# A transformer layer with split-precision weights: low parts in pieces, regrouped products, a third pair of split buffers and two moved buffers

## The reference

```
x = layer_norm(x, ...)                                   # "0"
h = x @ w_in + b_in                                      # iq, cbik, qa, kv, qb
out_a = swa_sink_attention(...); out_b = dsa_attention(...)   # top-k selection of keys
x = layer_norm(ALPHA * x + concat(out_a, out_b) @ w_o + b_o)  # "1"
x = layer_norm(ALPHA * x + memory_cross_attention(x, mem, ...))   # "2"
x = layer_norm(ALPHA * x + square(relu(x @ w_up + b_up)) @ w_down + b_down)   # "f"
u = rms_norm(x); x = x + ssd_mixer(u, ...)               # "r0"; 8 groups, 4 chunks each
u = rms_norm(x); x = x + mla_mixer(u, ...)               # "r1"; 16 heads, 8 pairs
return rms_norm(x)                                       # "r2"
```

## Time and profile before

| | |
|---|---|
| median of 3 runs | 1924.07 us (1923.3 to 1924.84) |
| the profiled execution | 1922.4 us, of which span 1920.6 us |
| mean granted PE clock | 0.959 of full speed |
| PE busy | 1763.4 us, 92% |
| PEld (weight loads, beside PE) | 1404.0 us, 73% |
| DVE, ACT, POOL busy | 950.1, 782.3, 621.2 us |
| chain that ended last | PE 72%, DVE 14%, ACT 8%, POOL 2%, issue 2% |

### The profile page before, as it was taken

The page is one execution under the profiler, slowest core; times in us unless marked ns, Lnnn a source line. Parts: engine busy times, 40 slices in busy tenths (PEclk is TensorE's granted clock), DMA queues, the critical chain, the costliest instruction groups (busy, mean ns, idle before and its releaser), DMA issues.

```text
span 1920.6 us, 22716 instructions
## 1 busy us (share of the span) xinstructions
PE 1763.4 (92%) x8994; PEld 1404.0 (73%) x8994; DVE 950.1 (49%) x1871; ACT 782.3 (41%) x1329; POOL 621.2 (32%) x223
## 2 busy tenths in 40 slices
PE   7895789889989999998888999999999999999998
PEld 6674465677778888887766777777778777777776
DVE  5157878353563221214655556345654354545455
ACT  5452343253264232322434444434444544443533
POOL 2323134212114434343124344434441313232320
PEclk9897789989989999999888999999999999999999
DMA  7222010112113222221121111121111212111111
GB/s 279 84 81 88 23 45 23 44 45 84 48 45 110 98 100 88 99 98 55 45 88 66 44 66 66 66 88 61 50 68 66 79 55 70 56 68 67 68 45 44
DMA packets 27408, 137.50 MB, mean 72 GB/s; under 512 B 2815, under 2 KB 9215, under 8 KB 13480
## 3 DMA queue, kind: packets, MB, share of 16 engines
q1 hardware_dynamic: 26248, 135.02, 19.9%
q10 hardware_dynamic: 1056, 1.05, 0.2%
HBM read 133.93 MB, written 2.12 MB: 71 GB/s over the span
## 4 chain that ended last, share of the span: by engine, by line
PE 72%; DVE 14%; ACT 8%; issue 2%; POOL 2%; DMA 1%; SPq 0%; DVEq 0%; ACTq 0%; POOLq 0%
PE ps L1184 70%; ACT whi L1588 2%; PE ps L1188 2%; POOL wlo L2531 1%; DVE STT L2439 1%; DVE XL L2021 1%; DVE SCB L2251 1%; DVE mx L2024 1%; DVE R L2021 1%; DVE m L2249 1%; ACT LG L1589 1%; ACT tmp L1588 1%; DVE tmp L2191 1%; ACT ESG L1588 1%; POOL tmp L2550 1%
## 5 line engine op out<-in xcount | busy, mean ns | idle before, releaser
L2531 POOL TENSOR_TENSOR wlo<-raw,whi 128x2048 fp32r<-128x2048 f32 (+3 forms) x123 | 527.4, 4288 | 1070.0 <-ACT whi L1588 1070.0
L1184 PE MATMUL ps<-XH,whi 128*128 128x512 f32 (+1 forms) x1144 | 446.1, 390 | 9.9 <-DVE XL L2021 4.5
L1184 PE MATMUL ps<-XH,wlo 128*128 128x512 f32 (+1 forms) x1144 | 425.6, 372 | 0.0
L1184 PE MATMUL ps<-XL,whi 128*128 128x512 f32 (+1 forms) x1144 | 425.3, 372 | 0.0
L1588 ACT ACTIVATE whi<-raw 128x2048 fp32r<-128x2048 f32 (+3 forms) x129 | 230.6, 1788 | 165.8 <-PE ps L1184 163.3
L1184 PEld LDWEIGHTS ps<-XH,whi 128*128 128x128 f32 x1144 | 221.2, 193 | 59.8 <-issue 16.5
L1184 PEld LDWEIGHTS ps<-XH,wlo 128*128 128x128 f32 x1144 | 220.8, 193 | 37.2
L1184 PEld LDWEIGHTS ps<-XL,whi 128*128 128x128 f32 x1144 | 221.4, 194 | 36.2 <-issue 2.2
L2121 DVE TENSOR_TENSOR R<-ps,R 128x512 f32<-128x512 f32 (+1 forms) x164 | 94.1, 574 | 288.2 <-PE ps L1184 287.4
L1184 PE MATMUL ps<-BH,whi 128*128 128x512 f32 (+1 forms) x608 | 227.8, 375 | 4.7 <-DVE BL L2461 2.0
L1184 PE MATMUL ps<-BH,wlo 128*128 128x512 f32 (+1 forms) x608 | 217.9, 358 | 0.0
(11 more groups left out here) (296 smaller groups left out, 2848.9 us busy)
## 6 DMA issues: line engine op xcount, KB each, us to landing
raw<-wall SPq DMA_DIRECT2D x108, 1024.0 KB, 4.6
raw<-wall SPq DMA_DIRECT2D x9, 512.0 KB, 3.3
raw<-wall SPq DMA_DIRECT2D x8, 576.0 KB, 3.4
raw<-wall SPq DMA_DIRECT2D x4, 768.0 KB, 4.0
R<-xT SPq DMA_DIRECT2D x1, 2048.0 KB, 13.2
BFL<-scr SPq DMA_DIRECT2D x16, 128.0 KB, 3.4
outT<-R SPq DMA_DIRECT2D x16, 128.0 KB, 1.9
MEM<-memT SPq DMA_DIRECT2D x2, 512.0 KB, 4.3
```

What stands on the lines that cost most here:

```text
L1184: return nc.tensor.matmul(o_, l, r_, start=start, stop=stop, skip_group_check=True)
L2531: tt(wlo[u % NSPL][:, 0:n], raw[u % NRAW][:, 0:n], f32(whi[u % NSPL][:, 0:n]), ALU.subtract).then_inc(S("g_lo"), 1)
```

## The change

Five edits.

1. `NSPL` goes from 2 to 3: a third pair `whi`/`wlo`. Since `split_first` runs over `NSPL` units, it now splits units 0, 1 and 2, all on DVE, and each later `split` is that of unit u + 2 at the place where it was that of u + 1.
2. The subtraction that makes `wlo` is done in pieces of 512 columns (384 where the unit is no multiple of 512), each with its own signal: four instructions for a unit of 2048 columns, on POOL and on DVE.
3. `pj` waits for `whi` alone at first, and for the piece of `wlo` that it needs ahead of each product that reads it. `right` waits for the high or the low part of the input, whichever the product reads.
4. The products of a part are regrouped. In mode "all": high by high for all k's, then high weights by low input for all k's, then low weights for all k's. In the other modes the low weights come ahead of the low input.
5. Addresses. `kv_at` is rounded up to 0 modulo 128, so that the buffers at its start (`KM`, `B2H`, `B2L`, `QCH`, `QCL` among them) begin at 0 modulo 128. `BTK0` and `IDR` move into the space of `RW`, and `st`, `m8` and `mx` into that of `KT`, to make room.

```
-NRAW, NSPL = 3, 2
+NRAW, NSPL = 3, 3
...
-        kv_at = top[0]
+        kv_at = top[0] = (top[0] + 127) // 128 * 128
...
+        def piece(u):
+            return 384 if units[u][1] % 512 else 512
+        def pieces(u):
+            return units[u][1] // piece(u)
...
-            "split": lambda u: ({"a_hi": 1, low[u]: 1}, []),
+            "split": lambda u: ({"a_hi": 1, low[u]: pieces(u)}, []),
...
-            def right(u, k, j):
+            def right(u, k, j, lo):
...
-                        e.wait_ge(*x_low(ep, jj, k))
-                    return XH[:, k, :], XL[:, k, :]
+                        e.wait_ge(*(x_low(ep, jj, k) if lo else on("a_xh", "nm", ep, jj, k // 3, i=k % 3 + 1)))
+                    return (XL if lo else XH)[:, k, :]
...
-                e.wait_ge(*on(low[u], "split", u))
                 h, l = weights(u, K)
                 c = slice(128 * m, 128 * m + 128)
-                for k in range(4 * part, min(4 * part + 4, K) if K == 8 else K):
-                    xh, xl = right(u, k, j)
-                    if key != "wk":
-                        xh, xl = xh[:, span(j)], xl[:, span(j)]
-                    t = three(o_, h[:, k, c], l[:, k, c], xh, xl, k == 0, k == K - 1)
+                ks = range(4 * part, min(4 * part + 4, K)) if K == 8 else range(K)
+                width = units[u][1] // K
+                def product(w, lo, k):
+                    x = right(u, k, j, lo)
+                    return mm(o_, w[:, k, c], x if key == "wk" else x[:, span(j)], k == 0 and w is h and not lo,
+                              k == K - 1 and (w is l if weights_last else bool(lo)))
+                def low_weights(k):
+                    e.wait_ge(*on(low[u], "split", u, i=((k + 1) * width - 1) // piece(u) + 1))
+                    return product(l, 0, k)
+                weights_last = mode == "all"
+                e.wait_ge(*on("a_hi", "split", u))
+                for k in ks:
+                    product(h, 0, k)
+                for last in range(2):
+                    for k in ks:
+                        t = low_weights(k) if weights_last == last else product(h, 1, k)
...
-                n = units[u][1]
+                n = piece(u)
                 e.wait_ge(*on("a_hi", "split", u))
-                tt(wlo[u % NSPL][:, 0:n], raw[u % NRAW][:, 0:n], f32(whi[u % NSPL][:, 0:n]), ALU.subtract).then_inc(S("g_lo"), 1)
+                for i in range(pieces(u)):
+                    c = slice(n * i, n * i + n)
+                    tt(wlo[u % NSPL][:, c], raw[u % NRAW][:, c], f32(whi[u % NSPL][:, c]), ALU.subtract).then_inc(S("g_lo"), 1)
```

More of the change, by code:

```diff
@@ L284, in program @@
         C = sb("C", [128, NCOL])
+        rw_at = top[0]
         RW = sb("RW", [128, NROW])
@@ L319, in program @@
         IW = sb("IW", [128, 4, 8])
-        st = sb("st", [128, 64])
-        m8 = sb("m8", [128, 8])
-        mxs = [sb(f"mx{i}", [128, 16]) for i in range(3)]
+        st = sb("st", [128, 64], at=kt_at + 2048)
+        m8 = sb("m8", [128, 8], at=kt_at + 2304)
+        mxs = [sb(f"mx{i}", [128, 16], at=kt_at + 2336 + 64 * i) for i in range(3)]
         QLS = [sb("QL0", [128, 4, 128]), sb("QL1", [128, 4, 128], at=b_at + 28672)]
@@ L364, in program @@
         XDE = [sb(f"XDE{i}", [128, 256]) for i in range(2)]
-        BTK = [sb(f"BTK{i}", [128, 128]) for i in range(2)]
+        BTK = [sb("BTK0", [128, 128], at=rw_at + 128), sb("BTK1", [128, 128])]
         CBM = [sb(f"CBM{i}", [128, 128]) for i in range(2)]
-        IDR = sb("IDR", [32, 32], F32R)
+        IDR = sb("IDR", [32, 32], F32R, at=rw_at)
         ACH = sb("ACH", [32, T], F32R, at=stat_at)
@@ L2043, in split @@
                     return
-                n = units[u][1]
+                n = piece(u)
                 e.wait_ge(*on("a_hi", "split", u))
-                tt(wlo[u % NSPL][:, 0:n], raw[u % NRAW][:, 0:n], f32(whi[u % NSPL][:, 0:n]), ALU.subtract).then_inc(S("d_lo"), 1)
+                for i in range(pieces(u)):
+                    c = slice(n * i, n * i + n)
+                    tt(wlo[u % NSPL][:, c], raw[u % NRAW][:, c], f32(whi[u % NSPL][:, c]), ALU.subtract).then_inc(S("d_lo"), 1)
             def xsum(k):
```

33 lines of the change are left out of this document (16 added, 17 removed).

## The result

The changed kernel takes 1893.86 us (median of 4 runs, 1893.39 to 1896.34) against 1924.45 for the kernel before on the same chip: ratio 0.9844, 95% interval 0.9827 to 0.9861. It is faster, by 30.6 us. The prediction said 1908 with a range of 1895 to 1920: the direction was right, the gain was about twice the forecast, and the median is 1.1 us outside the range. The profiled execution has a span of 1892.4 us, 28.2 less than before; the sum in the prediction had it 15.0 less. So 13 us are to be explained.

A forecast was written before the change was run, and what follows sets the result against it. PE, busy 92% of the span, was taken as the bound. Span 1920.6 - 21.2 - 5.5 + 11.7 + 2.0 + 1.0 - 3.0 = 1905.6 us, as median 1909.1, with unpriced small locks 1908; range 1895 to 1920.

The forecast's parts named there:

- Scan: DVE's decay product waits for one POOL piece, not a whole split; PE's waits and half clock shrink: -21.2 us.
- the alternation: In the scan's first group DVE and POOL take turns, one instruction each, whatever its length; basis of the 21.2 us.
- POOL keeps the port: Rival: in the scan, a waiting DVE instruction isn't let in between POOL's pieces; 1932 us, chance 0.09.
- given back: Rival: the chain through ACT behind the gated output paces the scan, half of 21.2 us lost; 1919 us, chance 0.12.
- Start: Third unit's split delays DVE's sums over x: PE's mean 9.7 us later, 2.0 us from half clock; +11.7 us.
- Regrouped products: On PE, as many products and weight loads, spacing 0.227 us whichever operand comes next, more waits: cost 0.
- Addresses: Products of 512 columns with moving operands now at 0 modulo 128 run 6.7 ns faster: -3 us, bounds -4 and 0.
- Norms: Four norms: each piece delays one DVE product, gain from waiting for `XH` alone is lost at the sums: +2.0 us.
- The clock: PE's half-clock work behind idle times: 6.8 us come back in the scan, 2.0 us are lost in the start.
- Attention: Less lock on DVE and a later POOL are of one size: +1 us, between -4 and +4.
- Third pair: PE's 4 waits for POOL's `wlo` go, all counted: -5.5 us, bounds 0 and 5.5.
- the start is not late: Rival: PE has other work ahead of the mean, or POOL's pieces miss the sums; 1896 us, chance 0.15.

The follow-up runs named there:

- e2: The changed kernel with each low part made in one instruction per unit again on both engines, all else kept: 1929.51 us, ratio to before 1.0022.
- e5: The kernel before with low parts in pieces of 512 (384) columns alone, PE still waiting for the last piece: 1905.35 us, ratio 0.9894.
- e7: The changed kernel with the third unit's split moved behind the sums over x, and pieces of 1024 columns (or half a unit): 1893.17 us.
- e4: The changed kernel with the three products of one k together again, waits for pieces of the low weights kept: 1900.13 us, ratio 0.9863.
- e9: The changed kernel with the third split behind the sums over x, and POOL's split held until DVE's last sum in three norms: 1873.74 us, ratio 0.9741.
- e10: The kernel before with the new product order alone: whole splits, two pairs, old addresses (some small buffers at new places): 1922.55 us, ratio 0.9984.
- e6: The changed kernel with kv_at left where it falls, at 64 modulo 128, nothing else changed: 1897.89 us.
- e3: The changed kernel with two pairs of split buffers instead of three, the third unit's split back on POOL: 1887.54 us, ratio 0.9794.

## Why the prediction was right in kind and wrong in size

**Scan: right.** -21.2 forecast, -21.7 measured; the alternation read from rows 4 decides. e2 and e5 show that the pieces alone bring it, e7 that it follows the size of a piece. "POOL keeps the port" and "given back" are refuted.

**Start: right** in mechanism and time of each step; 2.2 us too much. PE's product over the sums came 8.8 us late and not 9.7, and behind it 0.7 us more were lost and not 2.0: PE waited 5.5 us for the sums and not 12, having worked meanwhile, in part at half clock (0.83 on the mean over the first 36 us). **Regrouped products: right**, the spacing is unchanged. **Addresses: right in sum.** The 1.9 us between 564 and 886 agree with 288 products of 512 columns by 6.7 ns.

**Norms: the step that failed.** The lock of DVE behind POOL's split was priced as a gain in the scan alone. The prediction said: "By turns each of the four pieces delays one, so the queue's end is not earlier but later by POOL's added 0.5 us. What PE gains by waiting for `XH` alone it loses at the wait for the sums. Four such norms: +2.0." For norms 1 and 2 that is so (+0.05 for norm 1; e4, e9), though PE's wait for the sums of norm 1 is 3.87 us and not over 4, behind 3.0 us of waits for `XH`. I read norm 1 and carried it to all four, and between 886 and 937 that put +0.5 where, apart from the wait for `wlo`, the kernel gained 3.7. In norm f the chain is another one: DVE makes a tile of `R`, ACT squares it into `tmp`, PE adds it up, tile by tile, and there the kernel before had one more site of the kind that I counted only in the scan. Timeline of the kernel before at 909:

```profile
909.20 4.79 POOL L2531 TENSOR_TENSOR wlo<-raw,whi 128x2048 fp32r<-128x2048 f32 x1 [20.10 <-ACT whi L1588]
909.66 4.47 DVE L2017 TENSOR_SCALAR R<-R,C 128x256 f32<-128x256 f32 x1
914.69 2.08 PE L1184 MATMUL ps<-tmp,on1k 128*128 128x256 f32 x4 [4.08 <-ACT tmp L1588]
```

A DVE instruction that takes 0.35 us elsewhere took 4.47, and PE stood still for 4.08. The view of waits names ACT's `tmp` for it, so it hid in a group that I had not opened; only the name `STT` had led me to POOL. Product by product all six kernels of the experiments with pieces of 512 that keep POOL in this norm gain 3.2 us between 908 and 912, and so does the kernel after; the one with 1024 gains 2.1, the one with 256 3.8, and those with whole splits (e2, e10) nothing. So this step is the pieces' alone; what the parts share is what becomes of it afterwards. The gated output at 1043.78 is another such place. There DVE's `GY` took 3.13 us behind POOL's split of 1037.92, and PE's wait for `tmp` fell from 4.76 to 2.75: 2.0 us in every kernel with pieces of 512, none in e2 and e10. The kernel before, then the kernel after:

```profile
1039.83 3.13 DVE L2451 TENSOR_TENSOR GY<-GY,ZS 128x512 f32<-128x512 f32 x1
1043.78 3.75 PE L1184 MATMUL ps<-tmp,on 128*128 128x512 f32 x4 [4.76 <-ACT tmp L1588]
```

```profile
1037.70 1.12 DVE L2471 TENSOR_TENSOR GY<-GY,ZS 128x512 f32<-128x512 f32 x1
1039.63 0.67 PE L1190 MATMUL ps<-tmp,on 128*128 128x512 f32 x1 [2.75 <-ACT tmp L1606]
```

**The clock: a term that was mis-sized.** The prediction took 6.8 us back in the scan and lost 2.0 in the start. The mean granted clock rose from 0.959 to 0.966: as it is either full or half, PE was at half for 2 x 0.041 x 1920.6 = 157 us before and 2 x 0.034 x 1892.4 = 129 after, which is up to 14.4 us of work. In those stretches PE was at work for 109 us before and 89 after, so about 10 us came back, not 4.8. Norm f shows on how little it hangs. The kernel after and e4 have the same idle times there, e6 has 0.85 and 1.62 us. The two waits of the kernel after:

```profile
916.50 0.70 PE L1190 MATMUL ps<-tmp,on1k 128*128 128x256 f32 x2 [0.85 <-ACT tmp L1606]
919.18 0.70 PE L1190 MATMUL ps<-tmp,on1k 128*128 128x256 f32 x2 [1.97 <-ACT tmp L1606]
```

and of e4_old_order:

```profile
916.76 0.70 PE L1190 MATMUL ps<-tmp,on1k 128*128 128x256 f32 x2 [0.86 <-ACT tmp L1606]
919.43 1.22 PE L1190 MATMUL ps<-tmp,on1k 128*128 128x256 f32 x2 [1.98 <-ACT tmp L1606]
```

Busy time and, third from the end, the granted clock in the stretch behind them, of the kernel after, of e4 and of e6, one below the other:

```profile
918.70:928.70 10.00, 8.08 (x54) 6.97 (x54) 8.43 (x20) 5.04 (x12) 1.04 (x1) 1.00 0.30 105
```

```profile
919.00:929.00 10.00, 9.42 (x49) 8.72 (x50) 6.22 (x14) 3.75 (x9) 0.99 (x1) 0.68 0.31 107
```

```profile
919.60:929.60 10.00, 8.92 (x49) 8.13 (x50) 6.71 (x15) 4.00 (x10) 1.07 (x1) 0.76 0.31 105
```

Full clock in one, half for about six and five of the ten us in the others. What tips it the runs don't show. It goes with it that at this norm the pieces (3.1 us, e2), the order (3.3, e4) and the addresses (1.8, e6) each seem to be worth a good part of a gain of 4.95 in all, while order or pieces alone gain nothing there on balance: the parts are not additive. That the clock is the whole of it is not shown.

**Attention: the same step failed.** +1 was forecast, on the ground "Less lock on DVE and a later POOL are of one size"; -1.7 was measured, and +1.8 with whole splits. They were not of one size, and the gain is one more blocked instruction that I did not look for. It stands at 157 us, ahead of the long row of top-k instructions on DVE that PE waits for in the end, and its wait names POOL's `LG`. The kernel before:

```profile
156.00 4.61 POOL L2531 TENSOR_TENSOR wlo<-raw,whi 128x2048 fp32r<-128x2048 f32 x1 [6.26 <-ACT whi L1588]
157.11 3.65 DVE L2018 TENSOR_SCALAR SCB<-SCB 128x256 f32<-128x256 f32 x1
180.65 1.12 PE L1188 MATMUL ps<-KT,LG 128*128 128x128 f32 x4 [14.74 <-POOL LG L2555]
```

The kernel after:

```profile
166.23 0.71 DVE L2036 TENSOR_SCALAR SCB<-SCB 128x256 f32<-128x256 f32 x1
186.84 1.11 PE L1194 MATMUL ps<-KT,LG 128*128 128x128 f32 x4 [11.43 <-POOL LG L2577]
```

PE's wait is 3.3 us shorter. It is 11.4 us in every kernel with pieces of 512, 14.8 in e2 and e10, 12.5 with pieces of 1024 and 10.9 with 256. Half of the gain is lost again before 377, where e10, without pieces, loses 1.7 as well. The bound of -4 held.

**In sum**, the three blocked places that were not priced give 3.3 (attention), 3.2 (norm f) and 2.0 us (gated output) at the spot, and the clock 5 us more than forecast. These overlap with smaller losses elsewhere and do not add up to the 13.2 us exactly.

**Third pair**: of the 5.5 us of waits, all gone, part came back. The one near 510 us gave 1.15, and norm 2 was longer by 1.3. e3 leaves 0 to 3 us for the pair.

The range failed because it ended where "the start is not late" began (1896), as if that were the only way down. A range from bounds would have taken in the norms (down to -13) and the attention (down to -4), which the working named and the range did not use.

## What to carry to other kernels

Where an engine blocks another for the length of an instruction, search the trace for every instruction that is far longer than its line's shortest, on whatever chain, and price all of them; the wait's name shows only the last link. Cutting the long instruction frees a chain with one short victim (the scan), but in a queue full of victims it spreads the same loss over them, and there it must be moved out of the way (e9, 10 us). A buffer more, a signal more and a new order were worth little by themselves beside that in this kernel; ask of each what queue it passes (the third split ahead of the sums cost 9.7 us, and moving it was the cheapest gain of all). And compare kernels product by product: a sum over a stretch can hide a gain that the next stretch gives back (e2, at 1051).

## What the runs showed of the hardware

- DVE and POOL take turns, instruction by instruction, also between pieces of one kind: a waiting DVE instruction is let in at the end of each piece (25.29 to 32.9 and 390.55 to 396.5 above). The loss follows the piece: the decay product takes 4.44, 2.60 and 1.52 us at the longest with 2048, 1024 and 512 columns.
- A `TENSOR_SCALAR` on DVE with one tensor source, 128x256 fp32 in SBUF, was blocked as well (909.66, 4.47 us for 0.35; 157.11, 3.65 us for 0.36 at the shortest). The Trainium skill (SBUF — State Buffer, "Who interferes with whom") names this operation among those that can contend in a two-port mode. The trace agrees that it contends; in which mode it ran no trace shows.
- The product of 512 columns with the moving operand (the activations) at 0 modulo 128 takes 227 ns, at 64 modulo 128 233 (e6). With 256 columns it is the other way, 120 and 113 ns in the twelve products from 898 us on (e6).
- The granted clock stayed full behind idle times of 0.85 and 1.97 us in one kernel and fell to half behind 0.86 and 1.98 in another. At this place a forecast from the idle times alone would be 2 us off.
